# Expert blocks of a mixture-of-experts stage: 96 rows on four groups of 32 array columns, three weight buffers

## The chip, the cores and the metric

One core of one Trainium2 chip runs the kernel. The metric is the device time of one execution in microseconds (us); a version's time is the median of its runs. All arithmetic is f32.

## The reference

One inference step of a decoder layer for 1024 prompt rows and 8 sample rows of 1024 values. Two token mixers (sparse attention and a gated delta rule) are followed by a hierarchical mixture of experts, and only the latter is touched here:

```
logits  -> each row picks 1 of 4 groups, in it 2 of 8 experts, each with a weight
y[row] += weight * (silu(h[row] @ w_gate[e]) * (h[row] @ w_up[e])) @ w_down[e]     for its 2 experts e
```

There are 32 experts; `w_gate[e]` and `w_up[e]` are 1024 x 512 and `w_down[e]` is 512 x 1024, f32, so an expert has three times 2048 KB. The 1032 rows make 2064 pairs of row and expert.

## The kernel before

The mixers, the merge of their outputs (lines 2081 to 2086), the output projection with the router's logits (`block_out`) and the routing run one behind the other, each in a block that ends with a barrier of all engines. Then comes the stage of the experts.

**Routing** (`block_route`). VectorE ranks the pairs of every expert and gives each pair a slot: an expert's first 128 pairs go to block e, what is over goes to further blocks from 32 on. `tokens` holds each slot's row number (for the prompt and for the sample output), `slot_weight` its weight, `blocks` the expert of each further block and the number n of blocks in use. Meanwhile SP loads the weights of expert 0.

**Experts** (`block_experts`). A block is up to 128 rows of one expert. Its steps:
- GpSimd gathers the block's rows from `h2_rows` in HBM by an indirect DMA (L2525). An empty slot fetches a row of zeros.
- PE transposes them (L2563), ACT and DVE copy them out of PSUM as `xT` (L2599, L2619).
- PE computes gate and up: 2 x 8 products with a 128x128 piece of `xT` as the stationary operand and 512 columns of weights moving (L2572). Every f32 product is two instructions, each with a weight load of its own.
- ACT takes silu (L2603), DVE multiplies by up (L2623), PE transposes the result `a` (L2589), DVE copies it (L2634).
- PE computes down: 2 x 4 products of 512 columns (L2583). ACT and DVE scale the result with the slot's weight while they copy it out (L2610, L2630).
- GpSimd adds the rows to the outputs by two indirect DMAs (L2546), one for the prompt's rows and one for the sample's; slots with a row number out of bounds write nothing. It waits until both have landed, and only then takes the next block.

**Order.** `each_block` writes one order for all engines: in step b PE does gate and up of b, transposes the rows of b+1, does down of b-1 and transposes `a` of b. The loop goes over pairs of blocks, since the buffers alternate (`par`). SP (L2505 to L2512) waits until gate and up of the block before the last are done, issues gate and up of the next expert into that buffer, waits for down in the same way, and issues down. There are two buffers of weights, so a gate-and-up load is issued when gate and up of b end and is needed when gate and up of b+2 begin. All of SP's waits and loads are in one queue.

Of the kernel before, what the change touches and what calls it, by code (L numbers as in the profile page):

```python
# [21 lines left out]
P = 128  # L22
# [3 lines left out]
TS = 8  # L26
# [17 lines left out]
MAXBLK = 48  # L44
MAXOVER = 16
# [9 lines left out]
def constants():  # L55
# [47 lines left out]
    put("blk", np.tile(128.0 * np.arange(NT + 1), (P, 1)))  # L103
# [2153 lines left out]
def expert_weights(L, w_gate, w_up, w_down):  # L2257

    sem = L.signals.named("f_")
    gu_loaded, d_loaded = ([sem(n + str(i)) for i in range(2)] for n in ("gu_loaded", "d_loaded"))  # L2260
    W = [L.at(f"f_W{i}", A_W + 49152 * i, [P, 3 * 4096]) for i in range(2)]
    wg, wu = ([w[:, o:o + 4096].rearrange("p (k n) -> p k n", k=KD) for w in W] for o in (0, 4096))
    wd = [w[:, 8192:12288].rearrange("p (k n) -> p k n", k=4) for w in W]
    source = lambda w, e: w.rearrange("e (k p) n -> e p k n", p=P)[bass.ds(e, 1)].rearrange("a p k n -> (a p) k n")

    def load_gate_and_up(queue, par, e):
        for dst, w in ((wg[par], w_gate), (wu[par], w_up)):
            queue.dma_start(dst, source(w, e)).then_inc(gu_loaded[par], 16)  # L2268

    def load_down(queue, par, e):  # L2270
        queue.dma_start(wd[par], source(w_down, e)).then_inc(d_loaded[par], 16)  # L2271

    return wg, wu, wd, gu_loaded, d_loaded, load_gate_and_up, load_down

def block_route(nc, L, PS, C, logits, weight, tokens, slot_weight, blocks, weights):
# [6 lines left out]
    with ctx:  # L2283
        sem = L.signals.named("t_")
        step_sem, exp_in, exp_done, a_ready, rank_done, iota_done, iota_ready, hot_ready, table_done = map(
            sem, ("step", "exp_in", "exp", "a_ready", "rank", "iota", "iota_ready", "hot_ready", "table"))
# [13 lines left out]
        cmpb = Y("t_cmp", [P, NE, NT])  # L2300
# [3 lines left out]
        iota, blk128 = Y("t_iota", [P, P]), Y("t_blk128", [P, MAXBLK])  # L2304
        Z = Region(L, A_W + 49152, A_OA)
        hot, eq, val = Z("t_hot", [P, 2 * NT1, P]), Z("t_eq", [P, 2 * NT1, MAXBLK]), Z("t_val", [P, 2 * NT1, 2, MAXBLK])
# [5 lines left out]
        def _(dve):  # L2312
# [16 lines left out]
            V.tensor_scalar(eid128[:, :], C["eid"], float(P), None, ALU.mult)  # L2329
            V.tensor_scalar(blk128[:, :], C["blkid"], float(P), None, ALU.mult)  # L2330
# [30 lines left out]
            step(V.tensor_tensor(cmpb[:, :, :], count[:, :].unsqueeze(2).to_broadcast([P, NE, NT]), C["blk"][:, 1:NT1].unsqueeze(1).to_broadcast([P, NE, NT]), ALU.is_gt))  # L2361
# [8 lines left out]
            step(V.tensor_scalar(shift[:, :], shift[:, :], float(P), None, ALU.mult))  # L2370
            rank = PS[0][:, 0:NT1 * NE].rearrange("p (t e) -> p t e", e=NE)
            step(V.tensor_scalar(tmp[:, :, :], rank, float(P), None, ALU.is_ge))
# [6 lines left out]
            step(V.tensor_scalar(pos[:, :, :], slotf[:, :, :], 1.0 / P, 0.5 / P - 0.5, ALU.mult, ALU.add))  # L2379
            step(V.tensor_scalar(pos[:, :, :], pos[:, :, :], ROUND, None, ALU.add))  # L2380
            step(V.tensor_scalar(base[:, :, :], pos[:, :, :], -ROUND, float(P), ALU.add, ALU.mult))
# [4 lines left out]
            for i in range(PARTS):  # L2386
                r = slice(m * i, m * i + m)
                V.tensor_tensor(hot[:, r, :], iota[:, :].unsqueeze(1).to_broadcast([P, m, P]), posc[:, r].to_broadcast([P, m, P]), ALU.is_equal)
# [10 lines left out]
            V.tensor_scalar(tokens[:, 0:MAXBLK, 0], PS[3][:, 0:MAXBLK], float(TT), None, ALU.add)  # L2399
            step(V.tensor_scalar(far[:, :], PS[3][:, 0:MAXBLK], float(-TS), 4096.0, ALU.is_lt, ALU.mult))  # L2400
            V.scalar_tensor_tensor(tokens[:, 0:MAXBLK, 1], PS[3][:, 0:MAXBLK], float(TS), far[:, :], ALU.add, ALU.add)
            V.tensor_copy(slot_weight[:, :], PS[3][:, MAXBLK:2 * MAXBLK])

        @block.sync
        def _(sp):
            load_gate_and_up(sp, 0, 0)
            load_down(sp, 0, 0)

        @block.scalar
        def _(act):  # L2410
            act.wait_ge(iota_done, 1)
            nc.scalar.copy(iota[:, :], PS[2][:, 0:P]).then_inc(iota_ready, 1)
# [3 lines left out]
            nc.scalar.activation(ex[:, :, :], ex[:, :, :], ACT.Exp).then_inc(exp_done, 1)  # L2416

        @block.tensor
        def _(pe):
# [7 lines left out]
            for i in range(2 * NT1):  # L2427
                n = P if i < 2 * NT else TS
                if i % (2 * NT1 // PARTS) == 0:
                    pe.wait_ge(hot_ready, i // (2 * NT1 // PARTS) + 1)  # L2430
                ins = nc.tensor.matmul(PS[3][:, 0:2 * MAXBLK], hot[0:n, i, :], val[0:n, i, :, :].rearrange("p c b -> p (c b)"), start=(i == 0), stop=(i == 2 * NT1 - 1))
# [3 lines left out]
def block_experts(nc, L, PS, C, weights, h2_rows, tokens, slot_weight, blocks, y_p, y_s):  # L2435
# [4 lines left out]
    with ctx:  # L2440
        sem = L.signals.named("f_")
        counts_opened = sem("counts_opened")
        wg, wu, wd, gu_loaded, d_loaded, load_gate_and_up, load_down = weights

        (x_loaded, stored, gidx_ready, sidx_ready, tp_done, xT_act, xT_dve, gu_done, silu_done, a_done, atp_done,
         aT_done, down_done, out_act, out_dve, out_free, scale_ready) = ([sem(n + str(i)) for i in range(2)] for n in (
             "x_loaded", "stored", "gidx", "sidx", "tp", "xT_act", "xT_dve", "gu", "silu", "a", "atp",
             "aT", "down", "out_act", "out_dve", "out_free", "scale"))
        T = Region(L, A_HT, A_CONST)
        x = [T(f"f_x{i}", [P, D]) for i in range(2)]  # L2450
        xT = [T(f"f_xT{i}", [P, KD, P]) for i in range(2)]
        sg, a = T("f_sg", [P, FE]), T("f_a", [P, FE])
        aT = T("f_aT", [P, 4, P])
        out = [T(f"f_out{i}", [P, D]) for i in range(2)]
        scale = [T(f"f_scale{i}", [P, 8]) for i in range(2)]
        gidx, sidx = (L.at(f"f_idx{i}", A_W + 98304 + 416 + 32 * i, [P, 2, 2], I32) for i in range(2))
        block = ctx.enter_context(nc.Block())

        def each_block(engine, first=None, tail=None, rest=None):

            nothing = lambda *a: None
            first, tail, rest = first or nothing, tail or nothing, rest or nothing
            n = engine.value_load(blocks[0:1, MAXBLK:MAXBLK + 1], min_val=NE, max_val=MAXBLK)
            first(0, 1, 1, 0)
            rest(0, 1, 1)

            def step(b, par, i):
                first(par, i + 1 if par else i + 2, i + 2, b)  # L2470
                tail(1 - par, i + 1)
                rest(par, i + 1 if par else i + 2, i + 2)

            with engine.Fori(0, NE // 2 - 1) as i:
                step(2 * i + 1, 1, i)
                step(2 * i + 2, 0, i)
            step(NE - 1, 1, NE // 2 - 1)
            with engine.If(n < NE + 1):
                tail(1, NE // 2)
            with engine.If(n > NE):  # L2480
                with engine.Fori(NE // 2, MAXBLK // 2) as i:
                    for par, b, number in ((0, 2 * i, i + 1), (1, 2 * i + 1, i + 1)):
                        with engine.If(b < n):
                            first(par, number, i + 1 + par, b)
                        if tail is not nothing:
                            with engine.If(b < n + 1):
                                tail(1 - par, i + par)
                        if rest is not nothing:
                            with engine.If(b < n):
                                rest(par, number, i + 1 + par)  # L2490
                if tail is not nothing:
                    with engine.If(n > MAXBLK - 1):
# [235 lines left out]
```

## Time and profile before

| what | value |
|---|---|
| median of 3 runs | 2600.41 us (2597.03 to 2600.61) |
| span of the profiled execution | 2591.1 us |
| around the span, against the median | 9.3 us |
| PE busy | 2378.8 us, 92% |
| PE weight loads, DVE, ACT, GpSimd busy | 56%, 29%, 19%, 18% |
| DMA | 331.66 MB, mean 128 GB/s |
| stage of the experts | from 1856 us (first transposes) to the end |

In the timeline a bracket gives the engine's idle time ahead of the instruction and who ended it. The DMA share is the mean over 16 engines of the time their packets took, and can be a little over 1.

### The profile page before, as it was taken

Reading aid. Unit: us, or ns where it says so; the run is one execution under the profiler, and the core shown is the slowest. Engines: PE = TensorE matmul, PEld = TensorE weight load, DVE = VectorE, ACT = ScalarE, POOL = GpSimd, SP = SyncE. Lnnn points to the kernel's source line nnn. Section 1 sums busy time; section 2 is a strip of 40 time slices with the busy share of each in tenths; the row PEclk is TensorE's granted clock in tenths of the full one; section 3 lists DMA queues with packets and bytes.
Section 4 is the critical chain, followed back from the end, with each engine's and each line's share of the span. In section 5 each row is a group of like instructions: output and inputs, shape, how many; then the busy total and the mean of one; then the engine's idle time right before and its main releaser. Section 6 shows DMA issues by size and latency. Waiting matters only on the chain. (4 is left out here: it accounts for less than half of the span.)

```text
span 2591.1 us, 32776 instructions
## 1 busy us (share of the span) xinstructions
PE 2378.8 (92%) x12569; PEld 1440.9 (56%) x12569; DVE 745.9 (29%) x1524; ACT 489.3 (19%) x1335; POOL 461.8 (18%) x603
## 2 busy tenths in 40 slices
PE   8999998997879999699599999999499999999997
PEld 6456655886846656476366666544244444444443
DVE  2017343552656665344300000111411111111110
ACT  2111112332134555233100000001000000000000
POOL 1044121221401112200300000111012221222212
PEclk9999999998569999799799999999699999999999
DMA  5000300001300000655451000221679888889995
GB/s 172 33 33 33 140 2 1 2 2 38 67 2 2 1 2 2 163 164 151 126 163 33 33 1 33 60 90 58 225 283 323 313 314 314 313 314 321 316 320 160
DMA packets 185819, 331.66 MB, mean 128 GB/s; under 512 B 33989, under 2 KB 81614, under 8 KB 185486
## 3 DMA queue, kind: packets, MB, share of 16 engines
q1 hardware_dynamic: 161430, 293.38, 33.3%
q0 software_dynamic: 16096, 30.40, 4.1%
q10 hardware_dynamic: 8160, 6.07, 0.8%
q8 instruction: 88, 1.44, 0.2%
q14 instruction: 45, 0.37, 0.1%
HBM read 307.78 MB, written 51.37 MB: 139 GB/s over the span
## 5 line engine op out<-in xcount | busy, mean ns | idle before, releaser
L2572 PE MATMUL psum<-f_W,f_xT 128*128 128x512 f32 x1024 | 449.4, 597 | 7.6 <-DMA f_W<-w_up 6.6
L2572 PEld LDWEIGHTS psum<-f_W,f_xT 128*128 128x128 f32 x1024 | 193.0, 191 | 243.0 <-issue 231.6
L2081 PE MATMUL psum<-hT,x_wg 128*128 128x344 f32 x768 | 228.9, 457 | 4.3 <-DMA x_wg<-w_in 4.3
L2583 PE MATMUL psum<-f_W,f_aT 128*128 128x512 f32 x512 | 225.1, 592 | 1.1 <-DVE f_aT L2634 1.1
L398 PE MATMUL psum<-w,hT 128*128 128x512 f32 (+1 forms) x512 | 202.3, 553 | 0.0
L2081 PEld LDWEIGHTS psum<-hT,x_wg 128*128 128x128 f32 x768 | 147.4, 192 | 81.7 <-DMA x_wg<-w_in 4.4
L398 PE MATMUL psum<-hT,w 128*128 128x344 f32 x576 | 169.1, 454 | 0.0
L2583 PEld LDWEIGHTS psum<-f_W,f_aT 128*128 128x128 f32 x512 | 94.8, 190 | 108.5 <-issue 107.1
L398 PEld LDWEIGHTS psum<-w,hT 128*128 128x128 f32 x512 | 96.7, 192 | 97.2 <-issue 90.3
L2623 DVE TENSOR_TENSOR f_a<-f_sg,psum 128x512 f32<-128x512 f32 x32 | 22.0, 687 | 444.3 <-ACT f_sg L2603 444.3
L1618 ACT ACTIVATE a_P<-psum,a_nmax 128x512 f32<-128x512 f32 (+4 forms) x256 | 122.8, 493 | 125.7 <-DVE a_nmax L1536 85.4
L398 PEld LDWEIGHTS psum<-hT,w 128*128 128x128 f32 x576 | 108.6, 190 | 57.1 <-ACT dnT L449 0.9
L1532 DVE TENSOR_REDUCE a_nmax<-psum 128x2 f32<-128x1024 f32 (+4 forms) x128 | 91.0, 737 | 85.4 <-PE psum L1448 54.4
L2103 DVE TENSOR_TENSOR x_sig<-x_sig,psum 128x344 f32<-128x344 f32 x48 | 22.4, 509 | 319.5 <-ACT x_sig L2096 319.5
L2546 POOL DMA_INDIRECT out_y_prompt<-f_out,f_idx x32 | 51.1, 1598 | 301.1 <-DVE f_out L2630 156.2
L2603 ACT ACTIVATE f_sg<-psum 128x512 f32<-128x512 f32 x32 | 19.1, 597 | 443.0 <-PE psum L2572 443.0
L1465 PE MATMUL psum<-constants,a_P 128*128 128x128 f32 (+1 forms) x592 | 95.2, 287 | 0.7 <-ACT a_P L1618 0.5
L1445 PE MATMUL psum<-kT,qT 64*128 64x512 f32 (+3 forms) x384 | 83.4, 527 | 7.2 <-ACT a_P L1618 4.9
L2096 ACT ACTIVATE x_sig<-psum 128x344 f32<-128x344 f32 x48 | 19.3, 455 | 319.7 <-PE psum L2086 319.7
L1834 PE MATMUL psum<-constants,k_stage 128*128 128x128 f32 x384 | 61.4, 289 | 19.2 <-ACT k_T L1769 10.5
L2630 DVE TENSOR_SCALAR f_out<-psum,f_scale 128x512 f32<-128x512 f32 x32 | 24.0, 751 | 189.6 <-PE psum L2583 189.6
L1465 PEld LDWEIGHTS psum<-constants,a_P 128*128 128x128 f32 (+1 forms) x592 | 62.9, 141 | 23.3 <-issue 19.4
(511 smaller groups left out, 3241.7 us busy)
## 6 DMA issues: line engine op xcount, KB each, us to landing
f_W<-w_gate SPq DMA_DIRECT2D x32, 2048.0 KB, 14.8
f_W<-w_up SPq DMA_DIRECT2D x32, 2048.0 KB, 20.9
f_W<-w_down SPq DMA_DIRECT2D x32, 2048.0 KB, 9.5
k_stage<-cache_nsa SPq DMA_DIRECT2D x128, 192.0 KB, 2.5
w<-w_in SPq DMA_DIRECT2D x6, 2048.0 KB, 8.3
x_wg<-w_in SPq DMA_DIRECT2D x8, 1024.0 KB, 11.4
x<-x_prompt SPq DMA_DIRECT2D x8, 512.0 KB, 5.3
o_w<-w_out SPq DMA_DIRECT2D x2, 2048.0 KB
```

The costliest lines, as they stand in the source:

```text
L398: ins = nc.tensor.matmul(PS[i % 4][0:m_rows, 0:n], lhsT, rhs, start=(k == 0), stop=(k == KD - 1))
L1445: ins = nc.tensor.matmul(s[:, g, col:col + w], qT[rows, j, i * P:(i + 1) * P], key, start=True, stop=not masks)
L1465: ins = nc.tensor.transpose(bank[0:keys, x * P:(x + 1) * P], Pb[u % 2][:, g, at:at + keys], C["ident"])
L1532: ins = nc.vector.tensor_reduce(stats[:, c:c + 2], S[n % 2][:, :, col:col + width(part)], AX.X, ALU.max, negate=True)
L1618: ins = nc.scalar.activation(Pb[u % 2][:, g, o:o + w], S[n % 2][:, g, col:col + w], ACT.Exp, bias=nmax[:, u % 2, c0 + g:c0 + g + 1], accum ...
L1834: ins = nc.tensor.transpose(PS[4 + n % 2][:, k * P:(k + 1) * P], stage[s % 3][:, 4 * (q % 2) + k, q // 2, :], C["ident"])
L2081: ins = nc.tensor.matmul(PS[b + i][:, 0:n], wg[q % 3][:, k, i, c:c + P], hT[:, k, t0:t0 + n], start=(k == 0), stop=(k == KD - 1))
L2103: nc.vector.tensor_tensor(sg[u % 2][:, i, 0:n], sg[u % 2][:, i, 0:n], PS[4 * (u % 2) + 2 + i][:, 0:n], ALU.mult).then_inc(t_done, 1)
L2546: pool.indirect_dma_start(out=y, out_offset=bass.IndirectOffsetOnAxis(ap=sidx[:, par, c:c + 1], axis=0), in_=out[par][:, :], in_offset=Non ...
L2572: ins = nc.tensor.matmul(PS[bank][:, :], xT[par][:, k, :], w[par][:, k, :], start=(k == 0), stop=(k == KD - 1))
L2583: ins = nc.tensor.matmul(PS[5 + half][:, :], aT[:, k, :], wd[par][:, k, 512 * half:512 * half + 512], start=(k == 0), stop=(k == 3))
L2630: nc.vector.tensor_scalar(out[par][:, 512:1024], PS[6][:, :], scale[par][:, 0:1], None, ALU.mult).then_inc(out_dve[par], 1)
```

## The change

- A block has 96 slots (`SLOTS`), and up to 24 further blocks can be used. The routing arithmetic takes 96 for 128; `slot_weight` gets three copies, and rows 96 to 127 of it are filled by ACT.
- Every product of the experts is cut by rows: 32 of the 96 rows are the stationary operand and write 32 partitions of PSUM, so they use one of four groups of 32 array columns. In gate and up, groups 0 to 2 each take 32 rows against columns 0 to 383 of the weights, and group 3 takes the remaining 128 columns, for each of the three sets of rows in turn. `a` therefore is three pieces of 128 in place of four. In down, group 3 likewise takes the last 256 of the 1024 columns.
- DVE multiplies by the slots' weights before down (`weighted`) and no longer while it copies the output. The output comes out in three pieces on ACT and two on DVE.
- There are three buffers of weights, over a region that is free from the routing on; SP loads the experts 0, 1 and 2 in the routing block. The load of b waits for gate and up, and for down, of block b-3.
- The first 32 blocks are written out without a loop, with constants in the waits and the rows' indices read from `tokens` itself. PE's order is now gate and up of b, down of b-1, transposes of `a` of b, transposes of the rows of b+2. Scatter b waits for the landing of scatter b-1.
- The blocks from 32 on stand in `further`, a loop over 4 x 6 bodies, each under an `If`; there down of b follows in the same body, and GpSimd waits for a block's scatter before it passes on.
- The weights' transfers keep their form: runs of 2048 bytes for gate and up, of 4096 for down.

```diff
-MAXBLK = 48
-MAXOVER = 16
+SLOTS = 96
+NTHR = 10
+MAXBLK = 56
+MAXOVER = 24
...
-    gu_loaded, d_loaded = ([sem(n + str(i)) for i in range(2)] for n in ("gu_loaded", "d_loaded"))
-    W = [L.at(f"f_W{i}", A_W + 49152 * i, [P, 3 * 4096]) for i in range(2)]
+    gu_loaded, d_loaded = ([sem(n + str(i)) for i in range(3)] for n in ("gu_loaded", "d_loaded"))
+    W = [L.at(f"f_W{i}", A_R + 49152 * i, [P, 3 * 4096]) for i in range(3)]
...
-            load_gate_and_up(sp, 0, 0)
-            load_down(sp, 0, 0)
+            for e in range(3):
+                load_gate_and_up(sp, e, e)
+                load_down(sp, e, e)
...
+        def further(engine, each):
+
             n = engine.value_load(blocks[0:1, MAXBLK:MAXBLK + 1], min_val=NE, max_val=MAXBLK)
...
             with engine.If(n > NE):
+                with engine.Fori(0, (MAXBLK - NE) // 6) as i:
+                    for j in range(6):
+                        with engine.If(i * 6 + (NE + j) < n):
+                            each(i * 6 + (NE + j), (NE + j) % 3, j % 2, i * 2 + (NE + j) // 3 + 1, i * 3 + (NE + j) // 2 + 1)
...
+            def load(b, w, e):
+                sp.wait_ge(gu_done, b - 2)
+                load_gate_and_up(sp, w, e)
+                sp.wait_ge(down_done, b - 2)
+                load_down(sp, w, e)
+
+            for b in range(3, NE):
+                load(b, b % 3, b)
+
+            def each(b, w, par, wu_count, count):
+                load(b, w, sp.value_load(blocks[0:1, bass.ds(b, 1)], min_val=0, max_val=NE - 1))
+
+            further(sp, each)
...
+            def scatter_first(b):
+                pool.wait_ge(out_act, b + 1)
+                pool.wait_ge(out_dve, b + 1)
+                if b >= 1:
+                    pool.wait_ge(stored[1 - b % 2], 32 * ((b - 1) // 2 + 1))
+                scatter(b % 2, lambda c: tokens[slot, b, c:c + 1])
+
+            gather(0, tokens[slot, 0, 0:1])
+            gather(1, tokens[slot, 1, 0:1])
+            for b in range(NE):
+                pool.wait_ge(xt_done, b + 1)
+                gather(b % 2, tokens[slot, b + 2, 0:1])
+                if b >= 1:
+                    scatter_first(b - 1)
+            scatter_first(NE - 1)
+            pool.wait_ge(stored[1], 32 * (NE // 2))
+
+            def each(b, w, par, w_count, count):
+
+                pool.reg_mov(turn, b + 1)
+                done = pool.snap(turn)
+                pool.reg_mov(fetch, b - (NE - 1))
+                copied = pool.snap(fetch)
+                pool.wait_ge(xt_done, done)
+                nc.gpsimd.tensor_copy(gidx[slot, par, :], tokens[slot, bass.ds(b + 2, 1), :].rearrange("p b c -> p (b c)")).then_inc(gidx_ready, 1)
+                nc.gpsimd.tensor_copy(sidx[slot, par, :], tokens[slot, bass.ds(b, 1), :].rearrange("p b c -> p (b c)")).then_inc(sidx_ready, 1)
+                pool.wait_ge(xt_done, NE)
+                pool.wait_ge(gidx_ready, copied)
+                gather(par, gidx[slot, par, 0:1])
+                pool.wait_ge(out_act, NE)
+                pool.wait_ge(sidx_ready, copied)
+                pool.wait_ge(out_act, done)
+                pool.wait_ge(out_dve, done)
+                scatter(par, lambda c: sidx[slot, par, c:c + 1])
+                pool.wait_ge(stored[par], count * 32)
+                pool.sem_inc(scattered, 1)
...
+            def transpose_rows(b, par, count):
+                pe.wait_ge(x_loaded[par], 16 * count)
+                if not (isinstance(b, int) and b < 1):
+                    pe.wait_ge(xT_act, b)
+                    pe.wait_ge(xT_dve, b)
+                    ins = nc.tensor.transpose(PS[k // 4][:, (k % 4) * SLOTS:(k % 4 + 1) * SLOTS], x[par][slot, k * P:(k + 1) * P], C["ident"][slot, slot])
+                ins.then_inc(xt_done, 1)
+
+            def gate_and_up(b, w, par, w_count):
+                pe.wait_ge(xT_act, b + 1)
+                pe.wait_ge(xT_dve, b + 1)
+                pe.wait_ge(gu_loaded[w], 32 * w_count)
+                for m, bank in ((wg[w], 2), (wu[w], 3)):
+                        for t in range(3):
+                            nc.tensor.matmul(PS[bank][row[t], 0:NQ], xT[par][:, k, row[t]], m[:, k, 0:NQ], start=(k == 0), stop=(k == KD - 1))
+                        for t in range(3):
+                            ins = nc.tensor.matmul(PS[bank][row[3], P * t:P * t + P], xT[par][:, k, row[t]], m[:, k, NQ:FE], start=(k == 0 and t == 0), stop=(k == KD - 1 and t == 2))
+                ins.then_inc(gu_done, 1)
+
+            def transposes(b):
+                pe.wait_ge(a_done, b + 1)
+                for j in range(3):
+                    ins = nc.tensor.transpose(PS[4][:, j * P:(j + 1) * P], a[:, j, :], C["ident"])
+                ins.then_inc(at_done, 1)
+
+            def down(b, w, w_count):
+                pe.wait_ge(aT_done, b + 1)
+                pe.wait_ge(d_loaded[w], 16 * w_count)
+                if not (isinstance(b, int) and b < 1):
+                    pe.wait_ge(out_act, b)
+                    pe.wait_ge(out_dve, b)
+                part = lambda t, k: aT[:, k, row[t]] if k < 3 else aT[:, t, row[3]]
+                    for t in range(3):
+                        nc.tensor.matmul(PS[5][row[t], :], part(t, k), wd[w][:, k, 0:512], start=(k == 0), stop=(k == 3))
+                    for t in range(2):
+                        nc.tensor.matmul(PS[5][row[3], 256 * t:256 * t + 256], part(t, k), wd[w][:, k, 768:D], start=(k == 0 and t == 0), stop=(k == 3 and t == 1))
+                for k in range(4):
+                    for t in range(3):
+                        nc.tensor.matmul(PS[6][row[t], 0:256], part(t, k), wd[w][:, k, 512:768], start=(k == 0), stop=(k == 3))
+                    ins = nc.tensor.matmul(PS[6][row[3], 0:256], part(2, k), wd[w][:, k, 768:D], start=(k == 0), stop=(k == 3))
+                ins.then_inc(down_done, 1)
+
+            for b in range(2):
+                transpose_rows(b, b, 1)
+            for b in range(NE):
+                gate_and_up(b, b % 3, b % 2, b // 3 + 1)
+                if b >= 1:
+                    down(b - 1, (b - 1) % 3, (b - 1) // 3 + 1)
+                transposes(b)
+                transpose_rows(b + 2, b % 2, b // 2 + 2)
+            down(NE - 1, (NE - 1) % 3, (NE - 1) // 3 + 1)
+
+            def each(b, w, par, w_count, count):
+                gate_and_up(b, w, par, w_count)
+                transposes(b)
+                transpose_rows(b + 2, par, count + 1)
+                down(b, w, w_count)
+
+            further(pe, each)
...
+            def weighted(b, weight):
+                dve.wait_ge(silu_done, b + 1)
+                nc.vector.tensor_tensor(a[:, :, :], sg[:, :, :], PS[3][:, 0:NQ].rearrange("p (j n) -> p j n", j=3), ALU.mult).then_inc(prod_done, 1)
+                dve.wait_ge(prod_done, b + 1)
+                nc.vector.tensor_tensor(a[:, :, :], a[:, :, :], weight.to_broadcast([P, 3, P]), ALU.mult).then_inc(a_done, 1)
+
+            def copy_out(b, par, count):
+                dve.wait_ge(down_done, b + 1)
+                if not (isinstance(b, int) and b < 2):
+                    dve.wait_ge(stored[par], 32 * count - 32)
+                nc.vector.tensor_copy(out[par][slot, 512:768], PS[6][slot, 0:256])
+                nc.vector.tensor_copy(out[par][row[2], 768:D], PS[6][row[3], 0:256]).then_inc(out_dve, 1)
+
```

## Rows read from the trace of the kernel before

**Rows 1.** Page, part 2: slices of 64.8 us; digits tenths of busy time:

```profile
PE   8999998997879999699599999999499999999997
...
DMA  5000300001300000655451000221679888889995
...
GB/s 172 33 33 33 140 2 1 2 2 38 67 2 2 1 2 2 163 164 151 126 163 33 33 1 33 60 90 58 225 283 323 313 314 314 313 314 321 316 320 160
```

**Rows 2.** Windows: us, busy us (count) by engine, clock, DMA share, GB/s:

```profile
1946.20:2036.40 90.20, 89.02 (x244) 41.71 (x243) 10.55 (x16) 7.48 (x12) 19.34 (x26) 1.00 0.90 318
...
2397.20:2487.40 90.20, 89.19 (x243) 41.79 (x242) 10.54 (x16) 7.48 (x12) 18.62 (x24) 1.00 0.91 317
```

**Rows 3.** Groups of PE instructions by shape: xcount | busy us, mean ns:

```profile
L2572 PE MATMUL psum<-f_W,f_xT 128*128 128x512 f32 x1024 | 449.4, 597 | 7.6 <-DMA f_W<-w_up 6.6 <-ACT f_xT L2599 0.8
...
L2583 PE MATMUL psum<-f_W,f_aT 128*128 128x512 f32 x512 | 225.1, 592 | 1.1 <-DVE f_aT L2634 1.1
...
L2563 PE MATMUL psum<-constants,f_x 128*128 128x128 f32 x264 | 35.1, 277 | 6.9 <-DMA f_x<-h_rows,f_idx 6.9
...
L2589 PE MATMUL psum<-constants,f_a 128*128 128x128 f32 x128 | 19.3, 273 | 0.5 <-DVE f_a L2623 0.5
```

**Rows 4.** Page, part 4: the chain that ended last, by line:

```profile
DMA f_W<-w_up 11%; PE psum L2572 10%; PE psum L2583 5%; PE psum L2563 1%; SPq L2508 0%; SPq L2268 0%; SPq L2271 0%; DMA f_x<-h_rows,f_idx 0%; PE psum L2589 0%; POOL out_y_prompt L2546 0%; POOL out_y_sample L2546 0%; DVE f_a L2623 0%; ACT f_out L2610 0%; DVE f_aT L2634 0%; ACT f_sg L2603 0%
```

**Rows 5.** Timeline, PE: start us, us; work on four column groups:

```profile
48.33 1.18 PE L392 MATMUL psum<-w,hT 128*32 128x288 f32 x16
...
49.44 1.98 PE L398 MATMUL psum<-w,hT 128*128 128x512 f32 x4
...
1298.48 3.34 PE L1971 MATMUL psum<-v_stage,b_PT 128*8 128x128 f32 x115
```

**Rows 6.** Timeline, the end of the routing and block 0:

```profile
1850.38 0.18 POOL L2522 COPY f_idx<-tokens 128x2 int32<-128x2 int32 x1 [35.24 <-POOLq L2283]
...
1856.24 1.97 PE L2563 MATMUL psum<-constants,f_x 128*128 128x128 f32 x8 [6.87 <-DMA f_x<-h_rows,f_idx]
...
1859.04 16.64 PE L2572 MATMUL psum<-f_W,f_xT 128*128 128x512 f32 x32 [0.83 <-ACT f_xT L2599]
...
1876.35 0.69 DVE L2623 TENSOR_TENSOR f_a<-f_sg,psum 128x512 f32<-128x512 f32 x1 [17.41 <-ACT f_sg L2603]
...
1877.10 0.66 PE L2589 MATMUL psum<-constants,f_a 128*128 128x128 f32 x4 [0.54 <-DVE f_a L2623]
```

**Rows 7.** Windows with the weights' loads alone, and nearly alone:

```profile
1822.00:1834.00 12.00, 2.55 (x6) 1.85 (x6) 9.21 (x34) 0.21 (x1) 0.00 (x0) 0.50 1.04 393
...
1864.00:1872.00 8.00, 8.00 (x19) 3.49 (x18) 0.00 (x0) 0.00 (x0) 0.00 (x0) 0.97 1.04 398
```

**Rows 8.** DMA queues, 1946.2 to 2487.4: packets, MB, share of 16 engines:

```profile
q1 hardware_dynamic: 63095, 152.93, 78.1%
...
q0 software_dynamic: 10453, 18.80, 12.2%
```

**Rows 9.** DMA queue q0, 2549.6 to 2558.0 and 2481.9 to 2491.5:

```profile
q0 software_dynamic: 288, 0.44, 27.4%
...
q0 software_dynamic: 288, 0.40, 22.1%
```

**Rows 10.** Timeline, SP: two issues of a down load:

```profile
1819.67 3.75 SPq L2271 DMA_DIRECT2D f_W<-w_down  x1
...
1853.99 6.19 SPq L2271 DMA_DIRECT2D f_W<-w_down  x1
```

**Rows 11.** Lines 2525 (gather), 2546 (scatter): issue to landing:

```profile
DMA to landing us min/median/max: 4.5/7.0/8.6
...
DMA to landing us min/median/max: 4.3/8.5/9.3
```

**Rows 12.** Timeline, the last block's copy and scatter:

```profile
2576.61 0.75 DVE L2630 TENSOR_SCALAR f_out<-psum,f_scale 128x512 f32<-128x512 f32 x1 [7.33 <-PE psum L2583]
...
2578.33 1.56 POOL L2546 DMA_INDIRECT out_y_prompt<-f_out,f_idx  x1 [1.87 <-DVE f_out L2630]
```

More of the change, by code:

```diff
@@ L2456, in block_experts @@
-        gidx, sidx = (L.at(f"f_idx{i}", A_W + 98304 + 416 + 32 * i, [P, 2, 2], I32) for i in range(2))
+        gidx, sidx = (T(f"f_idx{i}", [P, 2, 2], I32) for i in range(2))
+        NQ = 3 * P
+        row = [slice(32 * t, 32 * t + 32) for t in range(4)]
+        slot = slice(0, SLOTS)
         block = ctx.enter_context(nc.Block())
-        def each_block(engine, first=None, tail=None, rest=None):
-            nothing = lambda *a: None
-            first, tail, rest = first or nothing, tail or nothing, rest or nothing
+        def further(engine, each):
@@ L2478, in each_block @@
-            with engine.If(n < NE + 1):
-                tail(1, NE // 2)
-            with engine.If(n > NE):
[L2481 to L2492, printed above, removed]
-                        tail(1, MAXBLK // 2)
+            with engine.If(n > NE):
+                with engine.Fori(0, (MAXBLK - NE) // 6) as i:
+                    for j in range(6):
+                        with engine.If(i * 6 + (NE + j) < n):
+                            each(i * 6 + (NE + j), (NE + j) % 3, j % 2, i * 2 + (NE + j) // 3 + 1, i * 3 + (NE + j) // 2 + 1)
@@ L2615, in _, with each @@
+            for b in range(2):
+                copy_rows(b, b)
+            for b in range(NE):
+                silu(b)
+                if b >= 1:
+                    copy_out(b - 1, (b - 1) % 2, (b - 1) // 2 + 1)
+                copy_rows(b + 2, b % 2)
+            copy_out(NE - 1, 1, NE // 2)
+            def each(b, w, par, w_count, count):
+                silu(b)
+                copy_rows(b + 2, par)
+                copy_out(b, par, count)
+            further(act, each)
         @block.vector
@@ L2640, in build, with each @@
+            copy_out(NE - 1, 1, NE // 2)
+            def each(b, w, par, w_count, count):
+                weighted(b, slot_weight[:, bass.ds(b, 1), :].rearrange("p b j -> p j b"))
+                copies(b)
+                copy_rows(b + 2, par)
+                copy_out(b, par, count)
+            further(dve, each)
 def build(nc, I, O):
```

221 lines of the change are left out of this document (74 added, 147 removed).

## The prediction

> **What bounds the kernel now.** I read the page's slices first: from slice 28 on PE is at 9 tenths and the DMA engines at 7 to 9, at some 315 GB/s [rows 1]; this is the stage of the experts, 1856 to 2578 us, and the change lies in it and in the routing ahead of it. The windows of four blocks each come next: 90.2 us for four blocks, PE busy 89.0 to 89.5 of them at clock 1.00, DMA share 0.90 [rows 2]. A block costs 22.55 us and PE has no idle time to give. The groups of PE instructions say what it is made of: 449.4 + 225.1 + 35.1 + 19.3 = 729 us over 32 blocks, 22.8 us a block, of which gate and up are 14.0 and down 7.0 [rows 3]. A 512-column f32 product is two instructions of 439 ns each. The chain of waits adds what the busy shares hide: the up weights' transfer stands in it with 11% of the span, beside PE's 10% and 5% [rows 4]. So two limits lie close together here: PE at 22.5 us a block and DMA not far under it. Whatever makes PE faster meets the other.
>
> **PE's work on a block after the change.** Four products that write four different groups of 32 array columns should run side by side. The trace of before has two places with just this. Line 392 puts 16 instructions (128x32 weights, 288 columns, four groups in turn) into 1.18 us; one after another at 288/512 of 439 ns they would need 3.95 us, so four run at once. Line 1971 runs 115 instructions of 128 columns on four groups in 3.34 us with a tail of 0.27, 27 ns each, 107 to 110 ns a round of four [rows 5]. An instruction of n columns then occupies its group for about n/128 x 107 + 2.5 ns.
> - Gate and up: per k and matrix, three groups each have 2 instructions of 384 columns (2 x 323 = 646 ns) and the fourth has 6 of 128 (6 x 109.5 = 657 ns). 16 k-steps x 657 = 10.5 us (14.0 before).
> - Down: 4 x max(2 x 430, 4 x 216) = 3.46 us, then 4 x 2 x 216 = 1.73 us: 5.2 us (7.0 before).
> - Transposes: 3 of 128 columns for `a` (0.6 us before for 4) and 8 of 96 for the rows (1.1 before): 0.45 + 0.85 us. Two changes a block between 32-column and full-array work: from line 392's first start to the next full-array product are 1.11 us, four rounds of 0.24 are 0.96 [rows 5], so I take 0.15 us each, 0.3 in all.
> Sum 17.4 us. Bounds: 16.9 (three quarters of 22.5) and, if the fourth group's instructions found no cover at all, 31 us (the slower rival). I take 17.4, because both rows with four groups show full overlap. Silu, two multiplications and the three-piece copies out are hidden: after gate and up of b, PE has down(b-1), 5.2 us, and one multiplication after silu took 0.7 us where nothing covered it [rows 6].
>
> **DMA's work on a block.** Three 2048 KB loads are 6.29 MB. With nothing else in the queues they ran at 393 GB/s, and at 398 with a little else [rows 7]: 16.0 us. The rest: in 24 blocks the weights' queue took 78.1% and the queue of gathers and scatters 12.2% of 541.2 us [rows 8], together 20.4 us a block in a measure in which full is 1.04 to 1.05 [rows 7], so 19.4 us. A gather of 96 rows in place of 128 saves 0.13 MB, 0.3 us. So **19.1 us a block**, of which 3.1 are gather, scatter and what they cost the weights. Lower bound: 6.95 MB at 393 GB/s, 17.7; upper: the 20.4 unscaled. I take 19.1, nearest to the steady rows. That is above PE's 17.4: DMA becomes the limit, and a third of the PE gain is lost in it. The 2048-byte runs and the order of rows are those of before and cost nothing.
>
> The Trainium skill (DMA: Bandwidth & Descriptors, Specifications) gives about 358 GB/s per core as the HBM limit. By that the weights alone would be 17.6 us a block, and the result about 50 us later. The trace disagrees with 393 and 398, so the sum doesn't use it.
>
> **Two more blocks.** A block takes 96 rows, and a scatter moves one 4 KB row per token. The scatters of two experts moved 0.44 MB and 0.40 MB in 288 packets [rows 9]: some 106 and 98 tokens, over 96 (the other 30 lie under). So n is 34 and two experts' weights come twice: 2 x 19.1 us of DMA, and two blocks in `further`, where down(b) no longer has the next gate and up before it.
>
> **Start.** SP now issues nine loads in the routing block, and SP's queue holds only so much: the third load's issue lasted 3.75 us, the one at 1853.99 6.19 us [rows 10]. At its end 1.26 MB of 6.29 had moved, so about 5.0 MB fit. The ninth issue ends when 13.9 MB have moved, 35.3 us after 1820.2: 1855.5. The block's end is a barrier that in the trace let GpSimd go at 1850.38 [rows 6]: now about +5 us. Two gathers beside a busy queue (7.0 median against 4.5 at least [rows 11]), rows(0) and rows(1) both ahead of the first product: gate and up of block 0 begin at 1868 instead of 1859.0. There the clock is at its lower level (granted 0.50 ahead of it, [rows 7]), as before (16.64 us for 32 instructions [rows 6] against 14.0: +2.7), so they end at 1881.7. Three experts and three gathers are in at 1871.5, and DMA idles 10 us until gate(3) may overwrite. Then gate and up of 3 until 1893; down(3) waits for down(0), which PE ends at 1885.5 + 10.7 + 5.2 = 1901.4: 8.4 us idle. A third buffer so gives DMA a start of 32 us and takes 18 back. From 1901.4 every buffer is free before its load is due (PE 17.4, DMA 19.1), and DMA runs on without a gap.
>
> **End.** From 1901.4: down(3) 5.3, experts 4 to 32 29 x 16.0 = 464, gate and up of 33 10.7, gathers and scatters 30 x 3.1 = 93: 2474.4. Gate and up of block 31 land two blocks earlier, 2436.2. PE: +10.7, down(30) 5.2, transposes 1.5, down(31) 5.2: 2458.8. Block 32: gate and up 2469.6; silu, products and transposes 2.9: 2472.5. Then PE stands before rows(34): GpSimd gathers them only after scatter(31) has landed, 2459.8 + 3.3 issue + 8.5 landing + 1, and 7.0 for the gather: 2479.6. Rows and down(32) until 2485.7. Block 33: 10.7 and 2.9: 2499.3; rows(35) wait likewise until about 2502; rows and down: 2508. The copies take 1.2, and from the last scatter's issue to the end of the span it was 12.8 us before [rows 12]: 2522. To this PE's lower clock after the two waits of some 7 and 3 us, 6 us, and GpSimd's passing of 22 `If` bodies not taken, 5 us (nothing to 12; no row prices it). **Span 2533**, against 2591.1 of the profiled execution: -58. The median of the runs, 2600.41, lies 9.3 us over that span: 2533 + 9 = **2542 us**.
>
> **Rivals.**
> 1. *PE stays the limit* (DMA at 17.7). Blocks 1 to 30 at 17.5: gate and up of 31 begin at 1885.5 + 525 = 2410.5 instead of 2436.2: 2516 us. For it: the 393 GB/s; against it: the windows of four blocks, in which a share of 0.90 moved 317 GB/s only [rows 2]. 0.17.
> 2. *DMA is dearer*, 20.4 us a block, as the raw shares are: 31 x 1.3 = 40 more: 2582 us. 0.15.
> 3. *The fourth group gets no cover* (slower). Both rows with four groups have equal lengths in all groups; here three groups hold 384 columns and the fourth three times 128 in turn. If the short ones wait for the long ones: 646 + 657 = 1.30 us per k, 20.8 for gate and up, 4 x (0.86 + 0.86) + 1.73 = 8.6 for down, 31 us a block: 1868 + 34 x 31 + 25 = 2947, some 2955 us. It decides from about 0.95 us per k. Against it: in line 1971 each f32 product is two instructions on one group; had the next group's first waited for both, only two groups would have run at once, 55 ns an instruction and not 27. 0.09.
> The Trainium skill (TensorE: Matmul & The Clock Gate, The mechanism) says that matmuls start and end strictly in program order; taken at its word, a short one may not end before a long one issued ahead of it, which is this rival. The trace's equal lengths can neither show nor refute it.
> 4. *PE's instructions come too slowly.* 550 a block instead of 120, one per 32 ns. Line 1971 kept two (weights and product) per 27 ns, but for 3 us only. At 21 us a block: 1868 + 34 x 21 + 25 = 2607, 2610 us or somewhat less. 0.07.
> That it doesn't do what it says (no row over 96, n = 32) is excluded by rows 9.
>
> **Numbers.** The forecast itself 0.52, with 2525 to 2560 as its own range. The range 2495 to 2595 takes in rival 1, most of rival 2, and leaves 3 and most of 4. Faster by over 0.2% (5 us, about what a measurement can tell) 0.84; within 0.03; slower 0.13.
>
> **What would show it.** In the middle, DMA share 1.03 or more in every window of four blocks, of 76 us, and PE busy at some 91% with its waits on f_W; gate and up spans of 10.5 to 10.7 us; 34 blocks, 32 + 2; gate(3) issued near 1882; PE waiting 5 to 8 us on f_x in block 32. It is wrong if blocks come at under 18 us (then PE is the limit, rival 1), if a gate-and-up span is over 12 us (3 or 4), or if the blocks 32 and 33 cost over 60 us together.

## The result, and the profile after

| | before | after |
|---|---|---|
| median of the runs, us | 2598.72 (2594.15 to 2600.61, 4 runs) | 2646.68 (2640.05 to 2647.14, 4 runs) |
| ratio | 1 | 1.0179, 95% interval 1.0163 to 1.0195 |
| span of the profiled execution, us | 2591.1 | 2638.4 |

The change made the kernel 1.8% slower; 2542 us and "faster" had been predicted. The page of the changed kernel first (slices of 66.0 us; compare [rows 1]), then the line of the instruction queue in the page of before:

```profile
PE   8999998997889998798599999995899998998710
...
PEclk9999999997689999899699999997899999999965
DMA  5000300001200001754610000225799999999600
GB/s 169 32 32 32 137 2 1 2 2 53 50 1 2 1 1 30 199 153 128 197 47 32 32 32 17 90 80 214 281 371 358 356 368 354 369 351 361 232 13 6
...
q8 instruction: 208, 3.41, 0.6%
```

```profile
q8 instruction: 88, 1.44, 0.2%
```

Before, PE was busy to the last slice. Now PE's last product ends at 2516 us, early in slice 39: the last two slices have PE at 1 and 0 and the DMA engines at 0. The stage itself did what was asked of it. The windows (us, busy us and count by engine PE, PEld, DVE, ACT, POOL, then clock, DMA share, GB/s) of four blocks each, early and late, and of the tail:

```profile
1893.40:1961.20 67.80, 67.80 (x1105) 58.29 (x1108) 11.97 (x25) 9.18 (x21) 15.25 (x12) 1.00 1.03 364
2092.90:2169.50 76.60, 72.43 (x1102) 62.91 (x1103) 11.72 (x24) 9.00 (x20) 13.96 (x12) 0.93 1.02 362
...
2363.90:2443.10 79.20, 71.34 (x1100) 61.84 (x1101) 11.92 (x24) 9.13 (x20) 13.83 (x12) 0.96 1.04 357
2520.00:2635.00 115.00, 0.00 (x0) 0.00 (x0) 0.00 (x0) 0.00 (x0) 1.51 (x2) 0.50 0.05 7
```

Four blocks took 90.2 us before [rows 2]. They take 67.8 while the head start of three loaded experts lasts, with PE busy all the time, and 76.6 to 79.2 after, with the DMA engines full. Then come 115 us in which no engine has anything to do that the profile counts, but for the issue of the last scatter (POOL, 1.51 us). The chain that ended last does not show them either. Its last steps (start us, us, what):

```profile
2510.85 0.42 PE psum L2587
...
2516.97 0.33 ACT f_out L2629
2517.35 0.38 ACT f_out L2630
2517.93 0.51 issue
2518.66 0.36 POOL out_y_prompt L2504
2519.03 1.38 issue
2520.41 1.41 POOL out_y_sample L2504
```

It ends with the last scatter at 2521.8 us, 117 us ahead of the end of the span. Where the pages are silent, the DMA queues of the window 2535 to 2635 have one thing (packets, MB, share):

```profile
DMA packets 41, 0.67 MB, mean 7 GB/s; under 512 B 0, under 2 KB 0, under 8 KB 0
## 3 DMA queue, kind: packets, MB, share of 16 engines
q8 instruction: 41, 0.67, 4.5%
```

Instructions are being fetched, in packets of 16 KB. The trace's own records of branches, which the page leaves out, tell for whom. The branches of TensorE's sequencer, each as start us, ns, line:

```
2514.8  4417 L2472    2519.4  4744 L2472    2524.3  4890 L2472    2529.4  4615 L2472    2534.1  5059 L2470
2539.4  4595 L2472    2544.1  4810 L2472    ... (16 more, 4545 to 5121)    2628.1  4924 L2472    2633.2  4619 L2472
2638.0    86 L2470
```

L2472 is the `If` over one block of `further`, L2470 its loop. Blocks 32 and 33 are executed; the 22 bodies behind them are not, and for TensorE each jump over one, and each jump back to the loop's head, costs 4.4 to 5.1 us: 25 of them, 119.1 us. The same branches take a median of 45 to 56 ns on the other four engines. The barrier at the block's end waits for TensorE. GpSimd, whose last branch is at 2531.0, with a drain of 4.88 us behind it, would have let the span end at 2536: within 3 us of the 2533 predicted. The other 102 us are TensorE's jumps.

### The profile page after: what moved, and what is told of

It is laid out like the page before. It is cut to its first block and busy times, and to the rows that moved or that the text cites. A ratio compares the mean times of both kernels' runs of the same rounds, so it can differ in the third digit from the quotient of the medians.

```text
span 2638.4 us, 47235 instructions
## 1 busy us (share of the span) xinstructions
PE 2267.6 (86%) x20007; PEld 1623.9 (62%) x20007; DVE 764.0 (29%) x1601; ACT 508.3 (19%) x1413; POOL 441.1 (17%) x515
## 3 DMA queue, kind: packets, MB, share of 16 engines
q1 hardware_dynamic: 166646, 305.97, 33.1%
## 5 line engine op out<-in xcount | busy, mean ns | idle before, releaser
L2567 PE MATMUL psum<-f_W,f_xT 128*32 128x384 f32 x3264 | 377.0, 506 | 40.2 <-DMA f_W<-w_up 37.2
L2569 PE MATMUL psum<-f_W,f_xT 128*32 128x128 f32 x3264 | 381.6, 281 | 0.1
L2569 PEld LDWEIGHTS psum<-f_W,f_xT 128*32 128x32 f32 x3264 | 365.6, 114 | 4.9 <-issue 0.3
L2567 PEld LDWEIGHTS psum<-f_W,f_xT 128*32 128x32 f32 x3264 | 148.1, 113 | 45.6 <-issue 37.2
L2656 DVE TENSOR_TENSOR f_a<-f_sg,psum 128x384 f32<-128x384 f32 x34 | 18.8, 554 | 413.1 <-ACT f_sg L2622 413.1
L2587 PE MATMUL psum<-f_W,f_aT 128*32 128x512 f32 x816 | 124.4, 597 | 0.7 <-DVE f_aT L2669 0.7
L2504 POOL DMA_INDIRECT out_y_prompt<-f_out,tokens x32 | 45.6, 1425 | 474.3 <-ACT f_out L2630 453.5
L2589 PE MATMUL psum<-f_W,f_aT 128*32 128x256 f32 x544 | 124.2, 382 | 0.0
L2622 ACT ACTIVATE f_sg<-psum 128x384 f32<-128x384 f32 x34 | 16.7, 490 | 395.5 <-PE psum L2569 395.5
L2589 PEld LDWEIGHTS psum<-f_W,f_aT 128*32 128x32 f32 x544 | 60.0, 111 | 33.5 <-issue 0.7
```

The costliest lines, as they stand in the source:

```text
L2504: pool.indirect_dma_start(out=y, out_offset=bass.IndirectOffsetOnAxis(ap=index(c), axis=0), in_=out[par][slot, :], in_offset=None, bounds_ ...
L2567: nc.tensor.matmul(PS[bank][row[t], 0:NQ], xT[par][:, k, row[t]], m[:, k, 0:NQ], start=(k == 0), stop=(k == KD - 1))
L2569: ins = nc.tensor.matmul(PS[bank][row[3], P * t:P * t + P], xT[par][:, k, row[t]], m[:, k, NQ:FE], start=(k == 0 and t == 0), stop=(k == K ...
L2587: nc.tensor.matmul(PS[5][row[t], :], part(t, k), wd[w][:, k, 0:512], start=(k == 0), stop=(k == 3))
L2589: nc.tensor.matmul(PS[5][row[3], 256 * t:256 * t + 256], part(t, k), wd[w][:, k, 768:D], start=(k == 0 and t == 0), stop=(k == 3 and t == 1))
```

## The experiments

The theory (T): a jump of TensorE to an instruction that it doesn't hold waits for its fetch, 4.8 us, and the count of such jumps is the loss. Rivals: the price goes by the length of the code passed (D), every forward branch has it (F), or the tail isn't TensorE's branches (O).

### Nested conditions

```diff
-                    for j in range(6):
+                    def nest(j):
                         with engine.If(i * 6 + (NE + j) < n):
                             each(...)
+                            if j < 5:
+                                nest(j + 1)
+                    nest(0)
```

> The six conditional blocks of one iteration of `further`'s loop are nested, so that the first one that fails skips the rest; nothing else differs. TensorE then takes some 4 forward branches over bodies not executed where the changed kernel takes 22. Theory (T): such a branch costs TensorE a fixed 4.4 to 5.1 us because its target isn't in the instructions that it holds; 4 or 5 of them remain, TensorE is through by about 2536 us, near the landing of the last scatter, and the time is 2546 us (2538 to 2560). Rival (D): the price goes by the instructions that are passed; the same code is passed, so about 2640 us. Rival (O): the tail after 2524 us is not TensorE's branches: about 2645 us.

Measured: 2545.53 us (2543.11 to 2551.73), ratio to before 0.9802 (0.9781 to 0.9823); span 2541.4. TensorE's records after its last product: 4592 ns (L2472), 4682 (L2470), then 234, 232, 215, 221, 215: it is through at 2535.5. Two long jumps are left in place of 25 (T had forecast four or five; its time is met), and the loop's further rounds cost next to nothing. O and D fall: the condition that fails first passes the code of four bodies in 4.6 us, and in the next round that of all six in 0.23. A few lines of control flow were the difference between 1.8% slower and 2.0% faster.

### Half the bodies

```diff
-MAXBLK = 56
-MAXOVER = 24
+MAXBLK = 44
+MAXOVER = 12
```

> Blocks allowed at most: 44 instead of 56 (12 bodies in `further` in place of 24, two of them taken; the routing's tables get smaller with them). T and D both: 10 bodies are passed in place of 22, 12 x 4.8 us less, 58 us: about 2588 us, and a few us less for the smaller tables in routing. O: about 2640 us, unchanged but for the tables.

Measured: 2601.66 us (2595.96 to 2605.03, 10 runs), ratio 1.0006 (0.9997 to 1.0016). TensorE's long jumps: 11, 52.8 us, in place of 25 and 119.1: 14 jumps fewer take 66 us away, where the forecast counted 12 and 58. But the result is 14 us over the forecast, so by the medians some 22 us have come in elsewhere, and 28 between the two profiled executions. The profiled execution shows where: its first load of the experts is issued at 1821.1 (1813.0 in the changed kernel's), and from the first gate and up to that of block 33 it takes 654 us in place of 636, at 341 to 355 GB/s. Both, 8 and 18 us, lie ahead of the jumps. The smaller tables gained nothing: 38.9 us from the first load's issue to the first gather, 37.3 in the changed kernel. The cause of the slower transfers is open.

### Shorter bodies

```diff
-                    for k in range(KD):
+                    for k in ks:
...
-                gate_and_up(b, w, par, w_count)
+                gate_and_up(b, w, par, w_count, (0, KD - 1))
```

> Leaves out k-steps 1 to 6 of gate and up in the blocks of `further` alone (144 of 192 products in each body; blocks 32 and 33 compute with a quarter of the sum). The count of branches is that of the changed kernel, the body that each passes falls from some 550 instructions to about 260. T (a far target has to be fetched, a near one not): the branches cost at most 0.4 us each, as TensorE's branch past 290 instructions in the kernel before did (382 ns); the time is 2525 us (2515 to 2540), 16 us of it the products left out. Rival F (every forward branch in a loop costs TensorE 4.8 us, whatever its length): about 2630 us. D (price by length): about half of each branch, 22 x 2.3 us: 2580 us.

> As the short body, but k-steps 2 to 5 are left out (96 of 192 products in each body in the blocks of `further`): some 360 instructions are passed by each branch. T with a window of instructions between the two lengths: either all of the branches cost 4.8 us or few of them do, some by where they lie; a mixture of short (under 0.5 us) and long ones would show a window that moves in steps. D: every branch some 3.1 us. No forecast of the count; the time between 2530 and 2640 us accordingly.

Measured: 2615.14 us (2611.38 to 2615.23) with two k-steps, 2625.99 (2622.97 to 2629.01, 2 runs) with four. None of the three numbers written down for the first came out. The records say why:

| kernel | long jumps (over 4.4 us) | short ones (2.8 to 3.5 us) | sum, us | instruction packets on the page |
|---|---|---|---|---|
| changed | 25 | 0 | 119.1 | 208 |
| four k-steps | 14 | 10 | 98.7 | 195 |
| two k-steps | 7 | 17 | 86.8 | 187 |
| 44 blocks | 11 | 0 | 52.8 | 180 |
| nested | 2 | 0 | 9.3 | 163 |
| nested, second profile (below) | 0 | 1 | 3.4 | 160 |

In the two kernels with shorter bodies one more jump, the first, took 0.38 to 0.39 us. There are two prices, not one by length (D) and not one for all (F). The queues of two windows of the kernel with two k-steps show what sets them, one short jump of 3.2 us (2541.9), and two long ones (2555.2 and 2560.3):

```profile
DMA packets 1, 0.02 MB, mean 5 GB/s; under 512 B 0, under 2 KB 0, under 8 KB 0
...
q8 instruction: 1, 0.02, 2.2%
```

```profile
DMA packets 4, 0.07 MB, mean 7 GB/s; under 512 B 0, under 2 KB 0, under 8 KB 0
...
q8 instruction: 4, 0.07, 4.4%
```

A short jump fetches one packet, a long one two. Count two for a long and one for a short jump, and take them off the page's packets: 158, 157, 156, 158, 159 and 159 are left in the six rows, the same to within 3. The packet records say it jump by jump: in the 12 profiles with this stage, each of the 61 jumps of 4.4 us and more has two packets within it, and each of the 33 of 2.8 to 4.0 us has one. So a jump that needs one new packet costs 3.1 us (mean of the 27 in the table's kernels with shorter bodies), two 4.8, none 0.2 to 0.4. T's condition (is the target held?) stands; its "short bodies are free" was wrong: with bodies of some 260 instructions 24 of 25 jumps still need a packet. No run has bodies so short that most of the jumps are free.

By the Trainium skill (Runtime: NRT & Kernel Launch, Instruction fetch mechanics) instructions come in blocks of 16 KiB and 256 instructions, two are held in sequence, and a taken branch out of them stalls until its target is fetched. The trace agrees: packets of 16 KB, at most two to a jump, and 0.2 to 0.4 us for a jump that fetches none.

The missing "16 us less" for the products left out is another matter. TensorE's waits from 2462 us on, in the changed kernel and in the one with two k-steps (us in total, times, longest):

```profile
PE psum L2557 <- DMA f_x<-h_rows,f_idx: 9.8, 1, 9.8
```

```profile
PE psum L2557 <- DMA f_x<-h_rows,f_idx: 24.7, 2, 17.3
```

The time that TensorE saved it stood waiting for gathered rows: 14.9 us more, for 16 saved. In these blocks of `further` the chain of GpSimd, scatter, its landing, then the gather, sets the pace.

### Two weight buffers

On the nested kernel, in short:

```diff
-    ... for i in range(3)] for n in ("gu_loaded", "d_loaded"))
+    ... for i in range(2)] for n in ("gu_loaded", "d_loaded"))
-                sp.wait_ge(gu_done, b - 2)
+                sp.wait_ge(gu_done, b - 1)
-                sp.wait_ge(down_done, b - 2)
+                sp.wait_ge(down_done, b - 1)
```

> The nested kernel with two weight buffers instead of three (two experts loaded during routing, the load of a block waits for the block two before it). What the third buffer is worth in the change, compared with the nested kernel's 2545.5 us. Theory: the transfers are the limit from block 8 on, and with two buffers the down load of one block and the gate and up loads of the next are still issued some 16 us into a block, in time to keep the DMA engines busy; it costs only the head start, 10 us (0 to 20): 2555 us. Rival: each load is issued late by its latency, 2 us a block, 60 us: about 2605 us.

Measured: 2579.49 us (2574.34 to 2583.77), ratio 0.9922 (0.9903 to 0.9942). The third buffer is worth 34 us (38 by the nested kernel's second measurement, 2541 us), between the two forecasts. Windows of four blocks in this kernel, then in the nested one (columns as above):

```profile
2099.80:2181.80 82.00, 72.40 (x1100) 62.81 (x1100) 11.92 (x24) 9.13 (x20) 15.15 (x12) 0.92 0.96 337
```

```profile
2116.20:2193.00 76.80, 71.31 (x1100) 61.88 (x1101) 11.07 (x23) 8.37 (x19) 15.15 (x12) 0.96 1.02 364
```

With two buffers the DMA engines pause, 0.96 instead of 1.02: 20.6 us a block from block 2 on. With three, the blocks up to 7 come at 16.9 and the rest at 19.7. From the first gate and up to that of block 31 that makes 629 us for 590: 5 blocks x 3.7 are the head start, 24 x 0.9 the fuller queues; routing, shorter by 4 us with two experts loaded, gives a little back. The theory had the first at half its size and missed the second.

### No down loads

```diff
                 load_gate_and_up(sp, w, e)
-                sp.wait_ge(down_done, b - 2)
-                load_down(sp, w, e)
```

> The nested kernel without the loads of the down weights after the first three (the blocks from the fourth on multiply with those of the first three). If the transfers set the pace from block 8 on, as in the prediction, all blocks come at TensorE's pace of 16.94 us, that of the changed kernel's blocks 1 to 7: gate and up of block 31 begin 65 us earlier, 2480 us in all (2470 to 2495). Rival: TensorE's own pace, with its clock falling after pauses, sets it: under 25 us less, over 2520 us.

Measured: 2468.54 us (2467.91 to 2473.17), ratio 0.9506 (0.9489 to 0.9523). Four late blocks:

```profile
2286.50:2354.20 67.70, 67.70 (x1101) 58.21 (x1100) 11.88 (x25) 9.11 (x21) 15.13 (x12) 1.00 0.88 293
```

This kernel computes wrong values, since the blocks from the fourth on multiply with old down weights; the time alone counts. It is 12 us under the forecast, just below its range. Blocks 2 to 31 each come at 16.9 us, with the clock at 1.00; gate and up of block 31 begin at 2388.1 and not at 2453.4, 65 us earlier as expected. Of 9 us more between the two profiled executions, 8 are in block 31 to 33, where no wait for gathered rows is left. The edit also takes out SP's wait for down; what speaks for the bytes and against this wait is the DMA share, 1.01 to 1.04 in the changed kernel and 0.88 here. The transfers hold the change at 19.5 us a block, and the lower clock (0.93 to 0.96) in the middle is a consequence of the pauses that they cause, not a limit.

### Gather ahead of the scatter's landing, and the third expert later

On the nested kernel, for the blocks of `further`:

```diff
-            pool.wait_ge(stored[1], 32 * (NE // 2))
...
+                pool.wait_ge(stored[1], NE // 2 * 32)
+                pool.wait_ge(stored[1 - par], (count - 1 + par) * 32)
+                pool.sem_inc(scattered, 1)
                 scatter(par, lambda c: sidx[slot, par, c:c + 1])
-                pool.wait_ge(stored[par], count * 32)
-                pool.sem_inc(scattered, 1)
```

> The nested kernel in which GpSimd, in the blocks of `further`, waits for the scatter before only ahead of its own scatter, and no longer ahead of the gather of the rows to come. TensorE's wait for rows(34) in block 32, 9.8 us in the changed kernel, goes; the clock stays up behind it. Theory: 10 to 15 us less than the nested kernel, 2533 us. Rival: the scatters still follow one another, and the chain of the last three scatters sets the end: under 4 us less, 2542 us or more.

In the next, also `range(2)` for `range(3)` in routing, and `load_gate_and_up(sp, 2, 2)`, `load_down(sp, 2, 2)` at the head of the experts' stage:

> As the one before (early gather), and the third expert's three loads are issued at the head of the experts' stage and not in routing. The barrier at routing's end no longer waits for SP's ninth issue: 4.5 us earlier, and with the first gather all blocks up to TensorE's limit. Theory: 4 us less than the early-gather kernel, 2529 us, the fastest of all. Rival: the transfers set the end, and nothing is gained by an earlier first gather: 2533 us.

Measured: 2535.58 us (2528.33 to 2546.83) and 2534.07 (2525.61 to 2537.84). The spreads were too wide to tell the two from each other, so all three ran again on one chip:

> The nested kernel again, five rounds, on one chip with the two that follow, since 2545.5, 2535.6 and 2534.1 us were measured on two chips with spreads of 9 to 18 us. Expected 2545 us, 0.980 of before.

> The early-gather kernel again. In its trace the wait for rows(34) is 4.9 us and block 32 to 33 takes 25.9 us from gate and up to gate and up (29.6 in the nested kernel): 4 us for block 32 and 1 for the end, so 5 us under the nested kernel: 2540 us. By the theory stated first (10 to 15 us) it would be 2533.

> Early gather and the third expert's loads after routing, again. Routing, from its first load's issue to the first gather, took 33.0 us in its trace and 38.3 in the early-gather kernel's: 5 us less than that one, 2535 us. Rival: the transfers set the end whatever the first gather does, no difference.

| kernel | median, us | ratio to before (95%) |
|---|---|---|
| nested | 2541.07 (2539.92 to 2547.28) | 0.9786 (0.9770 to 0.9801) |
| early gather | 2538.91 (2534.02 to 2543.81) | 0.9773 (0.9755 to 0.9790) |
| early gather, third expert later | 2533.29 (2528.32 to 2536.26) | 0.9743 (0.9728 to 0.9758) |

By the medians the early gather is not told apart from nothing; between the two profiled executions it is worth 4.8 us, near the 5 expected, but that is one pair. The wait in block 32 fell only from 8.9 to 3.5 us: scatter(31) itself is issued only when scatter(30) has landed, and gather(34) stands behind it. Both edits together gain 8 us (0.3%) over the nested kernel, 5.4 between the profiled executions. The barrier's end is where it was expected: 33.1 us from the first load's issue to the first gather, against 38.1 in the early-gather kernel. This kernel is 2.6% faster than before and, by the medians, 4.3% faster than the changed one.

## Why the prediction was wrong

The forecast was 2542 us; nested, with one or two fetching jumps in place of 25, the kernel is measured at 2541 and 2546. One step failed, in **End**: "GpSimd's passing of 22 `If` bodies not taken, 5 us (nothing to 12; no row prices it)".
- It asked the wrong engine. GpSimd went past its 22 bodies in 7 us, from the last landing at 2524.1 to 2531.0, much as said. But every engine goes through the same conditions, and TensorE's bodies are some 550 instructions each. The prediction knew that number (it is in rival 4) and used it only for the rate at which they are executed. TensorE's jumps took 119.1 us and put the end of the span 102 us behind GpSimd's.
- The bound was no bound. "Nothing to 12" had no row behind it. The trace before did have records: TensorE's branch past the whole of `n > NE`, some 290 instructions, took 382 ns, and its loop's branches 208. They would have misled too: 0.4 us times 25 is 10 us. What they don't hold is a jump that fetches packets; a fair upper end was a DMA round trip per jump, 7.0 us for a gather [rows 11]: 25 x 7.0 = 175 us. That end, with 2640 in the range, was missing, and so was the rival: two slower ones were listed, and neither was this.

The other steps, against the trace of after:
- **Four groups side by side.** Right, and rival 3 is refuted. The timeline of PE in block 3:

```profile
1910.34 0.52 PE L2567 MATMUL psum<-f_W,f_xT 128*32 128x384 f32 x3
1910.36 0.52 PE L2569 MATMUL psum<-f_W,f_xT 128*32 128x128 f32 x3
1910.68 0.50 PE L2567 MATMUL psum<-f_W,f_xT 128*32 128x384 f32 x3
1910.71 0.49 PE L2569 MATMUL psum<-f_W,f_xT 128*32 128x128 f32 x3
```

Three products of 384 columns and three of 128 begin every 0.33 us, two such a k-step: 655 ns. The three short ones begin 0.11 us apart, one behind the other on their group, while the long ones issued ahead of them keep the other groups for 0.33. Gate and up last 10.5 us as predicted, down 5.2 (5.2), the block 16.94 (17.4; its terms add up to 17.3). The Trainium skill (TensorE: Matmul & The Clock Gate, The mechanism) has all matmuls start and end in program order. The profile models the ends, so these rows can't show them; but the starts are not those of a short product that waits for the long ones, as rival 3 had it from that rule: by the pace, products of different column groups don't wait for each other's ends.
- **DMA.** 19.1 predicted. From block 9 to 31, (2443.1 - 2014.6) / 22 = 19.5 us, at 362 GB/s with a share of 1.01 to 1.04. Right as the limit, 2% short. Rival 1 would have needed 17.5; rival 2 had 20.4.
- **Two more blocks**: 34 blocks, as read from the scatters' bytes [rows 9].
- **Start.** The ninth issue, and the first gather:

```profile
1812.97 0.41 SPq L2270 DMA_DIRECT2D f_W<-w_gate  x1
...
1843.76 5.36 SPq L2273 DMA_DIRECT2D f_W<-w_down  x1
1873.59 0.37 SPq L2270 DMA_DIRECT2D f_W<-w_gate  x1
...
1892.36 0.37 SPq L2273 DMA_DIRECT2D f_W<-w_down  x1
```

```profile
1850.28 1.08 POOL L2499 DMA_INDIRECT f_x<-h_rows,tokens  x1 [40.74 <-POOLq L2285]
```

From the first load's issue to the first gather 37.3 us (32.8 before, +4.5 for the +5 of the text). All times lie 5.6 us earlier than predicted, because the stages ahead were that much faster in this execution. gate(3) came at 1873.6 where that shift makes 1876 of the 1882, down(3) at 1892.4 for 1896.
- **End.** gate and up of 31 began at 2443.1 (2436.2 predicted, 2430.6 with that shift: some 0.4 us a block more for the transfers); the wait for rows(34) was 9.8 us (7.1); the last scatter was issued at 2520.4. The signs asked for are there or near: shares of 1.02 to 1.04, 76.6 to 79.2 us, PE at 90 to 95% with 37.2 us of waits on f_W, in 16 pieces. One sign misled: a gate-and-up span of over 12 us was to speak for rivals 3 or 4, and block 0's and nine others are 12.3 to 13.5 us. In each of the nine the granted clock was at its lower level (0.50) for a part of the span, behind a pause of 1.7 to 4.0 us.

Right for the stage, wrong for the kernel: the last block's scatter is issued at 2518.7 for 2578.3 [rows 12], 60 us earlier, 54 of them from the stage; and a cost that was priced at 5 us took 102 more. That the rest of the sum is met within 3 us (2536 for 2533) is in part luck: the stages ahead were 5.6 us faster than in the trace of before, the transfers brought block 31 12.5 us late against that, and from there to GpSimd's end it took 4 us less.

## What to carry to other kernels

With bodies of some 550 instructions each jump over one, or back, cost TensorE 4.8 us, where the other engines paid 0.05: where unrolled bodies under a condition grow to hundreds of instructions, count the jumps that are taken, by engine, and nest the conditions so that the first that fails skips the rest. When a page shows a tail in which nobody works, look at the instruction queue's packets and the branches; the chain of waits does not hold them. A term that no row prices needs its upper end from the dearest like thing in the trace (here a DMA round trip) times the count on the engine with the longest code, not from the engine on the path.

## What was not expected of the hardware

- A jump that needs no fetch took 0.2 to 0.4 us on TensorE, 3.1 us with one packet of 16 KB, 4.8 us with two, while the DMA engines had next to nothing else to do. By the packet records, in one long jump of 4.75 us at 2554.0 the two began at 2554.6 and 2555.0 and took 1.6 and 1.9 us, so 1.8 us passed after the second; in the short one of 3.2 us at 2541.9 the packet began after 0.6 us and took 1.2.
- The same nested kernel had two long jumps on one chip (4.6 and 4.7 us) and, on another, one of 3.4 and one of 0.26 us; the last kernel had 5.1 and 4.7, then 3.6 and 0.27. Why is open; where the code lies may decide, and was not tried.
- Nearly the same stage ran at 341 to 355 GB/s in one program and at 356 to 370 in another, at shares of 1.0 both times: 19.5 to 20.0 us a block. No run here says what sets it. From the first gate and up to that of block 31 it makes 582 us in the changed kernel, 590 and 587 in the nested one and 598 with 44 blocks, each in one execution, so a difference of a few us between kernels can't be put down to their edits by one profile.
